# Expert weights in a ring of 16 tiles instead of 12, with TensorE and SyncE looping over four experts in a turn

## What is computed

```
def expert_chunk(args):
    toks, e = args
    hu = x_pad[toks] @ w_up[e] + b_up[e]             # w_up[e]   1024 x 2048: 8 MB
    return clamped_swiglu(hu) @ w_down[e] + b_down[e]  # w_down[e] 1024 x 1024: 4 MB
```

## Time and profile before

| | before |
|---|---|
| time, median of 3 runs | 1398.05 us (1396.36 to 1400.24) |
| the profiled execution: time / span | 1392.76 us / 1391.0 us |
| TensorE busy | 1186.3 us (85%) |
| VectorE / ScalarE busy | 309.0 us (22%) / 253.2 us (18%) |
| DMA, mean over the span | 334 GB/s |
| DMA in its steady stretches | 418 GB/s |
| granted TensorE clock, mean | 0.938 |

### The profile page before, as it was taken

The page is one execution under the profiler, slowest core; times in us unless marked ns, Lnnn a source line. Parts: engine busy times, 40 slices in busy tenths (PEclk is TensorE's granted clock), DMA queues, the critical chain, the costliest instruction groups (busy, mean ns, idle before and its releaser), DMA issues.

```text
span 1391.0 us, 20661 instructions
## 1 busy us (share of the span) xinstructions
PE 1186.3 (85%) x7931; PEld 582.3 (42%) x7932; DVE 309.0 (22%) x783; ACT 253.2 (18%) x370; POOL 0.2 (0%) x4
## 2 busy tenths in 40 slices
PE   4999899987977899998678777877787889799996
PEld 2745588835332334243234332333333333434432
DVE  1125454264111122121112111111111112103213
ACT  3035422112012111112111112111112020200211
POOL 0000000000000000000000000000000000000000
PEclk9999999997999999999899889987899999799998
DMA  9942475353779999989999999999999999955890
GB/s 335 380 154 90 177 262 212 137 213 152 278 267 419 416 417 418 418 356 420 418 416 417 418 418 418 418 418 416 417 419 418 418 418 417 415 198 181 337 415 34
DMA packets 102361, 464.79 MB, mean 334 GB/s; under 512 B 8124, under 2 KB 9364, under 8 KB 69430
## 3 DMA queue, kind: packets, MB, share of 16 engines
q1 hardware_dynamic: 100368, 461.52, 83.1%
q10 hardware_dynamic: 1958, 2.78, 0.6%
HBM read 463.22 MB, written 1.05 MB: 334 GB/s over the span
## 4 chain that ended last, share of the span: by engine, by line
PE 39%; DMA 19%; SPq 13%; issue 3%; DVE 2%; ACT 0%; DVEq 0%
PE psum L876 17%; DMA ring<-in_w_up 14%; PE psum L949 10%; SPq L485 7%; PE psum L826 6%; SPq L480 6%; DMA ring<-in_w_down 5%; PE psum L868 2%; PE psum L967 2%; DVE area L1540 1%; PE psum L912 1%; PE psum L851 1%; DVE area L1525 1%; PE psum L817 0%; DVE area L1563 0%
## 5 line engine op out<-in xcount | busy, mean ns | idle before, releaser
L876 PE MATMUL psum<-ring,area 128*32 128x512 f32 (+2 forms) x2432 | 413.1, 649 | 77.1 <-DMA ring<-in_w_up 77.0
L876 PEld LDWEIGHTS psum<-ring,area 128*32 128x32 f32 (+2 forms) x2432 | 101.9, 123 | 375.7 <-issue 227.6
L949 PE MATMUL psum<-ring,area 128*32 128x256 f32 (+1 forms) x2080 | 199.0, 422 | 26.5 <-DVE area L1525 14.8
L826 PEld LDWEIGHTS psum<-area 128*128 128x128 f32 x1056 | 131.4, 206 | 35.1 <-issue 35.1
L826 PE MATMUL psum<-area 128*128 128x128 f32 x1056 | 138.0, 292 | 0.3 <-DVE area L1470 0.3
L949 PEld LDWEIGHTS psum<-ring,area 128*32 128x32 f32 (+1 forms) x2080 | 71.7, 114 | 143.2 <-issue 79.6
L1500 DVE TENSOR_SCALAR area<-psum 128x256 f32<-128x256 f32 x51 | 21.6, 424 | 453.8 <-PE psum L876 453.8
L1138 ACT ACTIVATE area<-area 128x256 f32<-128x256 f32 x51 | 21.3, 417 | 443.3 <-DVE area L1500 443.3
L1126 ACT ACT_TABLE_LOAD x32 | 41.1, 1283 | 327.8 <-PE psum L851 327.8
L525 PE MATMUL psum<-hT,ring 128*128 128x256 f32 x370 | 83.6, 386 | 0.0
L525 PE MATMUL psum<-ring,hT 128*128 128x512 f32 (+1 forms) x192 | 77.8, 561 | 0.0
(11 more groups left out here) (177 smaller groups left out, 666.4 us busy)
## 6 DMA issues: line engine op xcount, KB each, us to landing
ring<-in_w_up SPq DMA_DIRECT2D x256, 1024.0 KB, 19.3
ring<-in_w_down SPq DMA_DIRECT2D x128, 1024.0 KB, 22.7
ring<-in_ada_w SPq DMA_DIRECT2D x12, 2048.0 KB, 16.6
ring<-in_w_in SPq DMA_DIRECT2D x11, 2048.0 KB, 19.6
ring<-in_w_out SPq DMA_DIRECT2D x2, 2048.0 KB, 10.2
ring<-in_w_branch_b SPq DMA_DIRECT2D x1, 2048.0 KB, 9.6
cst<-in_cst ACTq DMA_DIRECT2D x1, 1168.0 KB, 9.4
x_res<-in_x SPq DMA_DIRECT2D x1, 1024.0 KB, 5.1
```

Of the source, the lines that this page charges most:

```text
L826: ins = pe.matmul(ps[banks[i]][:, kk % 4 * P:(kk % 4 + 1) * P], h2[:, tt, kk * P:(kk + 1) * P], S[:, tt, 0:P], start=(tt == 0 and kk % 4 = ...
L876: ins = pe.matmul(ps[b][g * P // G:(g + 1) * P // G, 0:w], XT[:, kk, t0:t0 + P // G], wt[:, c0:c0 + w], start=False, stop=kk == KT - 1, sk ...
L949: ins = pe.matmul(ps[b][g * M:(g + 1) * M, 0:w], hidT[:, p, q * P + of * M:q * P + (of + 1) * M], down_weights(kk)[:, g * W + d * CW:g * W ...
```

## The change

The ring gets 16 places: the 12 tiles of `ring` and the four places named above. Tile i of expert e stands in place (12e + i) mod 16, so that the places repeat after four experts. `freed(e, i)` says which use makes a place free: the first four tiles of expert e go where the down tiles of expert e-2 or up tiles four back in the ring stood, and so on, 16 tiles behind. What stood in the four places is moved: `posm64` into `rope`, `kept` into the attention masks in `cst`, a piece of `arena` and `silu_router`.

A tile's address now depends on the expert's number mod 4, and addresses are fixed in the code. So TensorE's loop holds the code of four experts, `pe0` to `pe3`, each with all seven bodies; `experts(..., each=4)` writes the four near bodies one behind the other in the loop, and then the 24 far bodies behind it. SP's loop also covers four experts. VectorE and ScalarE still loop over one expert.

```diff
+TILES, PLACES, AROUND = 12, 16, 4
...
-        ybT = sb("ybT", 4 * T)
+        ybT_b_down = sb("ybT_b_down", 4 * T + D)
...
-        kept = xn[:, :].rearrange("p (b n) -> p b n", n=CW)
...
-        posm64 = region(0, (TT, E + 1))
+        posm64 = rope[:, 0:TT * (E + 1)].rearrange("p (t e) -> p t e", t=TT)
+        kept = [cst[:, C_MASK:C_MASK + CW], cst[:, C_MASK + CW:C_MASK + 2 * CW], arena[:, 13824:13824 + CW],
+                silu_router[:, :]]
...
+        def place(j, i):
+            return (TILES * (j % AROUND) + i) % PLACES
+
+        def tile(j, i):
+            n = place(j, i)
+            if n < TILES:
+                return slot(NF + n // 2)[:, n % 2 * 2 * D:(n % 2 + 1) * 2 * D]
+            return (hT[:, :], arena[:, 0:2 * D], xn, ybT_b_down[:, :])[n - TILES]
...
-                rest = one(nc.snap(i, min_val=0, max_val=E - 1), root)
-                nc.regs_add(i, i, 1)
+                e = nc.snap(i, min_val=0, max_val=E - each)
+                rest = []
+                for j in range(each):
+                    rest += one(e + j if j else e, j, root)
+                nc.regs_add(i, i, each)
...
+            def freed(e, i):
+                if i < 3:
+                    return dn_used, 3 * (e - 2) + i + 1
+                if i < 4:
+                    return dn_full, MAX_D * (e - 1)
+                if i < 4 + KT - 2:
+                    return up_used, (KT - 2) * (e - 1) + i - 4 + 1
+                return up_full, MAX_U * e
...
+            for e in range(1, AROUND):
+                for i in range(TILES):
+                    if e == 1 and i == 0:
+                        b, n = un.place["hb11"]
+                        sp.wait_ge(bank_full[b], n + 1)
+                    elif e == 1 and i == 3:
+                        sp.wait_ge(acc_done, 1)
+                    elif e > 1 or i > 3:
+                        sp.wait_ge(*freed(e, i))
+                    load(e, e, i)
...
-            with sp.Fori(1, E) as e:
+            with nc.body("sp_loop", valid_engines=only):
+                e0 = nc.snap(n, min_val=AROUND, max_val=E - AROUND)
+                for j in range(AROUND):
+                    e = e0 + j if j else e0
+                    for i in range(TILES):
+                        sp.wait_ge(*freed(e, i))
+                        load(e, j, i)
...
-            experts(pe, "pe", lambda e, root: [by_class(pe, pe.value_load(cls_i[0:1, ds(e, 1)]), lambda k: body(e, k), "pe", root)])
+            experts(pe, "pe", lambda e, j, root: [by_class(pe, pe.value_load(cls_i[0:1, ds(e, 1)]), lambda k: body(e, j, k),
+                                                 f"pe{j}", root)], AROUND)
```

More of the change, by code:

```diff
@@ L204, in layer_kernel @@
         cls_i = sb("cls_i", E + 1, I32)
+        ybT = ybT_b_down[:, 0:4 * T]
+        b_down_sb = ybT_b_down[0:E, 4 * T:]
+        silu_rep = silu_router[:, 0:KT * 32]
+        w_router_sb = silu_router[:, KT * 32:]
         xn = area[:, 0:TT * D]
@@ L306, in layer_kernel @@
         ld_gain = [sem("ld_gain1"), sem("ld_gain2")]
-        up_tile = [sem(f"up_tile{i}") for i in range(KT)]
-        dn_tile = [sem(f"dn_tile{i}") for i in range(FT // 2)]
+        tile_in = [[sem(f"tile_in{h}_{i}") for i in range(TILES)] for h in range(2)]
         up_used, dn_used = sem("up_used"), sem("dn_used")
@@ L409, in layer_kernel, with up_weights, down_weights @@
         names = sorted(where, key=where.get)
[L411 to L416, removed]
+        def place(j, i):
[5 more added lines that the diff above has]
+            return (hT[:, :], arena[:, 0:2 * D], xn, ybT_b_down[:, :])[n - TILES]
+        def up_weights(j, kk):
+            return tile(j, kk)
+        def down_weights(j, kk):
+            return tile(j, KT + kk // 2)[:, kk % 2 * D:(kk % 2 + 1) * D]
         def by_class(eng, cls, body, tag, root):
@@ L441, in by_class, with experts @@
             return others()
-        def experts(eng, tag, one):
+        def experts(eng, tag, one, each=1):
             only = [eng.engine]
@@ L487, in _, with load @@
[L487 to L494, removed]
-            with sp.Fori(1, E) as e:
[L496 to L507, removed]
+            def load(e, j, i):
+                if i < KT:
+                    src = a["w_up"][0][ds(e, 1), i * P:(i + 1) * P, :]
+                    sp.dma_start(tile(j, i), src.rearrange("e p n -> p (e n)")).then_inc(tile_in[j % 2][i], 16)
+                else:
+                    src = a["w_down"][0][ds(e, 1), (i - KT) * 2 * P:(i - KT + 1) * 2 * P, :]
+                    sp.dma_start(tile(j, i).rearrange("p (k n) -> p k n", k=2),
+                                 src.rearrange("e (k p) n -> p (e k) n", p=P)).then_inc(tile_in[j % 2][i], 16)
@@ new lines, in _ @@
+            for e in range(1, AROUND):
[8 more added lines that the diff above has]
+                    load(e, e, i)
+            only = [sp.engine]
+            n = nc.alloc_registers("sp_i", engines=only)
@@ new lines, in _ @@
+            nc.regs_mov(n, AROUND)
+            nc.br("sp_loop", engines=only)
+            with nc.body("sp_loop", valid_engines=only):
+                e0 = nc.snap(n, min_val=AROUND, max_val=E - AROUND)
+                for j in range(AROUND):
+                    e = e0 + j if j else e0
+                    for i in range(TILES):
+                        sp.wait_ge(*freed(e, i))
+                        load(e, j, i)
+                nc.regs_add(n, n, AROUND)
+                nc.br_lt(n, E, "sp_loop", "sp_end", engines=only)
@@ L508, in _ @@
+            nc.switch_bb("sp_end")
             for tt in range(TT):
@@ L833, in _, with body, arrived_tile @@
             gathers(FIRST_BANKS, 1)
-            def body(e, k):
+            def body(e, j, k):
+                def arrived_tile(i):
+                    pe.wait_ge(tile_in[j % 2][i], 8 * e + 16 - 8 * (j % 2))
                 passes, units = PASSES[k], up_units(k)
@@ L884, in body @@
                 for kk in range(last):
[L885 removed]
+                    arrived_tile(kk)
                     for u in range(n_u):
@@ L1144, in _ @@
             experts(act, "act",
-                    lambda e, root: [by_class(act, act.value_load(cls_i[0:1, ds(e, 1)]), lambda k: body(e, k), "act", root)])
+                    lambda e, j, root: [by_class(act, act.value_load(cls_i[0:1, ds(e, 1)]), lambda k: body(e, k), "act", root)])
             act.wait_ge(acc_done, E + 1)
@@ L1541, in body, with expert @@
                         at += 1
-            def expert(e, root):
+            def expert(e, j, root):
                 cls = v.value_load(cls_i[0:1, ds(e, 1)])
```

26 lines of the change are left out of this document (10 added, 16 removed).

## The result

| | before | after |
|---|---|---|
| time, median | 1397.2 us (1394.06 to 1400.24, 4 runs) | 1477.78 us (1472.66 to 1480.32, 4 runs) |
| ratio, 95% interval | | 1.0572 (1.0535 to 1.061) |
| span of the profiled execution | 1391.0 us | 1475.1 us |
| granted TensorE clock | 0.938 | 0.906 |

The account below looks back on a forecast made before the run. It took DMA (experts 9 to 25) and TensorE (ahead and behind) to bound the kernel in turn. Terms 15.8 + 2.1 + 31.7 - 0.5 made +49.1 on 1392.8, so 1441.9, with 5.3 for the median 1447 us; range 1402 to 1482.

Parts of the forecast that it names:

- What bounds the kernel: DMA limits experts 9 to 25, at 2.51 us a tile; TensorE is the limit ahead of that and behind it.
- the ring: Four more tile places put DMA 10.0 us ahead and close a 3.9 us hole: -14.4 us by themselves.
- Which branches stall: New TensorE stalls on absent code: seven in experts 4 to 8, four in 22 to 25, five in 26 to 31.
- The sum of 49.1: Whole kernel: 15.8 us late after the early experts, 2.1 at experts 22 to 25, 31.7 at the end, less 0.5.
- the price: Each TensorE branch to an absent code block: 4.1 us taken, from 4.1 to 6.0, plus 2.8 an expert for the clock.
- Experts 4 to 8: Six stalls counted in four experts, 6 x 4.1 + 4 x 2.8 = 35.8 us; loads end 15.8 late.
- Experts 22 to 25: Four stalls, 16.4 us, against waits for tiles of 14.3: 2.1 us, with the slow clock left to the waits.
- Tail: Experts 26 to 31, all TensorE: five stalls and four slow clocks, 31.7 us, less 0.5.
- The upper bound of the prediction: All stalls at 6.0 us: +77.6, so 1475.7 us, up to 1487 if experts 22 to 25 pay for the clock.
- B: TensorE stalls few, as its store holds more blocks or returns find blocks fetched early: 1396 to 1412 us; chance 0.16.
- C: TensorE branches cost little, or the seen stalls have another cause, so only the added places count: 1383.7 us; chance 0.16.
- D: The added tile places fail to help while TensorE's stalls come: 1462 to 1490 us; chance 0.08.

Follow-up runs that it names:

- Code4_ring12: The kernel before with four copies of the seven bodies in TensorE's loop, the ring kept at 12 places and buffers unmoved: 1499.02 us.
- code2_ring12: The kernel before with two copies of the bodies in TensorE's loop, the ring kept at 12 places: 1468.14 us.
- before_far_moved: The kernel before with TensorE's far bodies reordered, so that far1 and far2 stand 2,495 instructions further from the loop: 1448.97 us.
- after_small_loads: The changed kernel with each load of an expert's tile cut to 128 columns, so that DMA is nearly idle during the experts: 1362.89 us.
- staged_once: The kernel before with marked returns and moved buffers; GpSimd copies expert 1's tiles 0 to 3 from the four freed places into the ring of 12: 1390.44 us.
- staged_each: The kernel before with marked returns and moved buffers; tiles 0 to 3 of every expert pass through the four freed places and GpSimd's copies: 1385.04 us.

## Why the prediction was right in direction and short in size

**What bounds the kernel, and the ring: right.** Experts 1 to 3 take 10.7 us less (10.0 predicted). Code4_ring12 shows the ring's worth at nearly equal code, 21.2 us: more than the 14.4 of the sum. I put that to the holes that open when TensorE stalls; no run separates it.

**Which branches stall: right.** All that I had named stalled: expert 4 twice, 5, 6, 7 twice, 8, 22 to 25, 26, 27, 28 twice, 29, 31; q8 had 98 packets (80 to 120 predicted). Those between 9 and 21 (16, 17, 18, 20, some 6 us each) were hidden: the lag at expert 12 was 39.1 us and at expert 21 40.3.

**The sum of 49.1 against 84.1: 35.0 short**, and the step that failed is the price: "I take 4.1 for the stall, not 6.0, because most of these branches are of the first row's kind, in a stretch where the ring is full and DMA rests". By terms:
- Experts 4 to 8, 35.8 predicted. The seven stalls added 39.0 us of idle time, 5.6 each, where six at 4.1 make 24.6. With 39.4 + 10.7 = 50.1 for the whole stretch, 11.1 is left for the lower clock, 2.2 an expert (2.8 for each of four predicted). That term was right: TensorE is busy 167.8 us in 477.0 to 680.6 after and 156.4 us in 468.0 to 633.1 before, 11.4 more for the same 1,162 matmuls, at a mean granted clock of 0.90 against 1.00. The price was 4.1 where DMA rested, but the ring of 16 keeps DMA at work, so that it didn't rest: expert 5's stall is 4.76 us at a share of 0.19 with 12 places and 6.48 at 0.57 with 16, and expert 27's is 4.73 at 0.19 and 6.52 at 0.37. So the change made its own stalls dearer. The seventh, at expert 8, I had left out of this stretch.
- Start to expert 1: nothing predicted, 8.1 measured. Expert 0's branch to far2 had 2.35 and has 5.33, and I had counted its stall as unchanged; three more near bodies now stand between the choice and far2. Some 4 us lie ahead of it; in the kernels tried here expert 0 starts anywhere from 343.0 to 352.9, so I put no cause to them.
- Experts 9 to 20 gave back 7.3, not 10.0.
- Experts 22 to 25: 2.1 predicted, 11.0 measured. The stalls are 5.6 to 6.7 us with DMA full. Whether the clock that I had left to the waits is paid too, no run separates.
- Tail: 31.2 predicted (31.7 - 0.5), 32.8 measured. Expert 29's stall was cheap (4.11), the others dear.

In all: 8.1 + (50.1 - 35.8) - (10.7 - 10.0) + (10.0 - 7.3) + 8.9 + 1.6 = 34.9, which is the 35.0 but for rounding. So 8.1 of the 35.0 lie ahead of expert 1, where the sum had nothing. The upper bound of the prediction, 6.0 for all, came to 1475.7, close to the 1477.8 measured; that is partly luck, for it has neither the 8.1 nor the seventh stall.

**Rivals.** B (few stalls) and C (faster) fall by 22 stalls. D falls by the 61.2 us. The Trainium skill ("Advanced Engine Details and Errata", section ISA Cache) states 128 KB on TensorE and lines of 16 KB, which comes to 8 lines. The stalls that the prediction lists for the changed kernel came out by a store of that size, with one block fetched ahead and the longest unused going out, two things that the page doesn't state; the counts for code2_ring12 and before_far_moved did not, with some 5 and at least 7 stalls more than counted.

## What to carry to other kernels

Code is a working set. Before copying a loop's body to fix addresses, count blocks of 256 instructions over everything that runs in turn, rare branches too, and keep what runs often in one contiguous piece. Such a count is rough: it was too low for two of the kernels here, so measure q8's packets. Where a branch goes to code that can't stay, mark it early so that the block comes while the engine works: on returns alone that took some 46 of 80.6 us back. And price a fetch under the DMA load that the change itself will make, not under the load of the trace before.

## What the runs showed of the hardware

- The idle time behind a branch of TensorE to an absent block was 3.0 us (expert 25, after_small_loads) to 5.0 us (expert 1, before) with DMA at rest and 5.6 us (expert 23, after) to 7.4 us (expert 6, before_far_moved) with DMA full; a branch back to the loop's start took 6.2 to 6.8 us in both (after, after_small_loads).
- A branch marked ahead takes at most 1.1 us (0.81 ahead of expert 5, 1.07 ahead of expert 1 in the kernel before), as one to present code does (0.98).
- Behind a stall TensorE is granted the lower level, 1.2 GHz, for its first products: 1.94 us for 8 products of the class 0 body against 1.06, behind the short stall of expert 29 (4.11 us) as behind the long ones.
- The same seven bodies in another order cost anything from -7 to +54 us.
- GpSimd copied 128x2048 fp32 in 1.9 us (staged_once, staged_each).
